# Gated-delta heads of a hybrid decoder step: the next head's convolutions, gates and norms are issued among the present head's work

## What is computed

```python
def causal_conv(u, buf, w):
    ...
    out = sum(xp[:, i:i + l] * w[i] for i in range(CONV_W))
...
    g = jnp.cumsum(log_a, axis=-1)
    diff = g[..., :, None] - g[..., None, :]
    decay_strict = jnp.exp(jnp.where(strict, diff, -jnp.inf))
    decay_causal = jnp.exp(jnp.where(causal, diff, -jnp.inf))
    kb = k * beta[..., None]
    lower = jnp.einsum('nbhik,nbhjk->nbhij', kb, k) * decay_strict
    a_mat = lower + jnp.eye(c, dtype=lower.dtype)
    ...
    sol = lax.linalg.triangular_solve(a_mat, rhs, left_side=True, lower=True)
    ...
    def step(s, xs):
        ...
        v_new = u_c - jnp.einsum('bhik,bhkv->bhiv', w_c, s)
        o = jnp.einsum('bhik,bhkv->bhiv', qd_c, s) + jnp.einsum('bhij,bhjv->bhiv', qk_c, v_new)
        s = s * gl_c[..., None, None] + jnp.einsum('bhjk,bhjv->bhkv', kd_c, v_new)
        return s, o
```

## Time and profile before

| | |
|---|---|
| median of 3 runs | 2871.9 us (2869.86 to 2873.43) |
| profiled execution | 2865.93 us, span 2864.2 us |
| PE busy | 2749.2 us, 96% of the span |
| DVE, POOL, ACT busy | 49%, 32%, 14% |
| chain of waits by engine | PE 85%, DVE 10%, ACT 2%, issue 2% |

### The profile page before, as it was taken

How to read it: one execution, slowest core, us unless ns; L and a number is a source line. 1 busy time by engine, 2 the same in 40 slices (tenths; PEclk the granted TensorE clock), 3 DMA queues, 4 the chain that set the end, 5 groups by cost and what they waited for, 6 DMA issues and landing times.

```text
span 2864.2 us, 42850 instructions
## 1 busy us (share of the span) xinstructions
PE 2749.2 (96%) x17350; PEld 2649.3 (92%) x17350; DVE 1411.2 (49%) x2523; ACT 406.7 (14%) x716; POOL 923.5 (32%) x1227
## 2 busy tenths in 40 slices
PE   8989889999999999999999999998999999999997
PEld 7877777898999999999999999997899999999997
DVE  5765756555576144261465335445575153261443
ACT  4333333222230000000001011112220000000001
POOL 3321221223234333333433323223233333343341
PEclk9999999999999999999999999999999999999999
DMA  3110110112311111111122122112311111111112
GB/s 125 52 53 16 53 53 16 60 53 69 107 38 45 47 50 45 45 52 45 45 65 91 51 67 77 54 52 76 106 35 47 45 48 49 45 45 52 45 45 74
DMA packets 46300, 160.22 MB, mean 56 GB/s; under 512 B 7198, under 2 KB 9118, under 8 KB 45102
## 3 DMA queue, kind: packets, MB, share of 16 engines
q1 hardware_dynamic: 30528, 111.20, 13.1%
q10 hardware_dynamic: 15598, 46.43, 4.5%
HBM read 138.97 MB, written 18.64 MB: 55 GB/s over the span
## 4 chain that ended last, share of the span: by engine, by line
PE 85%; DVE 10%; ACT 2%; issue 2%; DMA 1%; POOL 0%; DVEq 0%; ACTq 0%; POOLq 0%; SPq 0%
PE proj L376 71%; PE bank L453 10%; DVE s L899 2%; PE proj L431 1%; PE bank L450 1%; DVE s L797 1%; DVE x_lo L839 1%; DVE s L915 1%; PE bank L440 1%; DMA w_raw<-w_all 0%; PE bank L672 0%; DMA small<-rows_c 0%; DVE s L898 0%; DVE s L907 0%; DVE s L1016 0%
## 5 line engine op out<-in xcount | busy, mean ns | idle before, releaser
L376 PE MATMUL proj<-x_hi,w_hi 128*128 128x344 f32 x4716 | 1549.2, 328 | 54.2 <-DVE s L797 32.0
L376 PE MATMUL proj<-x_lo,w_hi 128*128 128x344 f32 x4716 | 1518.4, 322 | 0.0
L376 PE MATMUL proj<-x_hi,w_lo 128*128 128x344 f32 x4716 | 1517.8, 322 | 0.0
L376 PEld LDWEIGHTS proj<-x_hi,w_hi 128*128 128x128 f32 x4716 | 897.0, 190 | 79.2 <-issue 60.9
L376 PEld LDWEIGHTS proj<-x_lo,w_hi 128*128 128x128 f32 x4716 | 897.5, 190 | 1.6
L376 PEld LDWEIGHTS proj<-x_hi,w_lo 128*128 128x128 f32 x4716 | 896.8, 190 | 0.0
L311 POOL TENSOR_TENSOR w_lo<-w_raw,w_hi 128x256 fp32r<-128x256 f32 x808 | 665.2, 854 | 16.2
L307 POOL TENSOR_TENSOR pool_gate<-pool_gate 1x1 f32<-1x1 f32 x204 | 53.2, 261 | 1886.2 <-PE proj L376 1839.1
L1254 DVE TENSOR_TENSOR h<-h,proj 128x344 f32<-128x344 f32 x144 | 73.9, 513 | 453.1 <-PE proj L376 453.1
L1244 DVE TENSOR_TENSOR mlp_t<-proj,rbc 128x344 f32<-128x344 f32 x192 | 99.1, 516 | 269.6 <-PE proj L376 252.6
L308 POOL CAST w_hi<-w_raw 128x1024 fp32r<-128x1024 f32 x202 | 209.0, 1034 | 0.0
(11 more groups left out here) (270 smaller groups left out, 1900.6 us busy)
## 6 DMA issues: line engine op xcount, KB each, us to landing
w_raw<-w_all SPq DMA_DIRECT2D x204, 512.0 KB, 3.6
h<-x SPq DMA_DIRECT2D x8, 516.0 KB, 9.1
s<-rows_a ACTq DMA_DIRECT2D x8, 516.0 KB, 4.7
h<-x ACTq DMA_DIRECT2D x8, 516.0 KB, 6.9
h_spill<-h ACTq DMA_DIRECT2D x8, 516.0 KB, 2.6
h<-h_spill ACTq DMA_DIRECT2D x8, 516.0 KB, 6.6
y<-h ACTq DMA_DIRECT2D x8, 516.0 KB
sample_C<-state_c ACTq DMA_DIRECT2D x4, 1024.0 KB, 6.6
```

The costliest lines, as they stand in the source:

```text
L376: last = nc.tensor.matmul(PJ[:, tt, 0:TT], w[slot][:, k, :], x[:, k, tt * TT:(tt + 1) * TT], start=(at == 0 and j == 0), stop=(at == len(o ...
```

## The change

The delta heads become a pipeline of two. `mixer_ab` is split into `retention`, `delta_front` and `delta_main`. The front (26 steps: taps, silu, gate, norms) of head h+1 is issued among the places of the main part of head h, by a second table `DELTA_FRONT`; head 0's front is issued during a prologue of 12 places with 8 projection steps each. The projection stream is one generator over all delta tiles, two tiles further ahead than before: two tiles, then 96 steps in the prologue, 96 in each of heads 0 to 2, and 48 in the last head (`DELTA_LAST_FILL`), where before each of the four heads had 96 and four tiles stood ahead of them. The tiles of a head come in the order q, k, v, gate. Odd heads keep their convolved rows in other buffers (s[8] and two slices of the mixer output) than even heads.

Inside the head: the product of k and beta and the scaling of v by beta are gone; beta multiplies the triangular matrices (L1034 of the new program) and the new values of the scan (L1096) instead. The turned v is copied by ACT rather than by DVE. The causal mask is a constant of 0 and -200 that the exponents' instruction takes as a third operand (L1024), in the mLSTM heads too, where L1126 goes. The newest tap of q moves from DVE to ACT. The products of q with exp(g) move to level 2 of the inversion on DVE. The next head's decay row is loaded, and the sample states too, at level 2 on ACT; the beta rows are loaded once for the samples only. ACT loads function tables twice per head, before three times.

The core of the diff (lines that only rename are left out):

```diff
-DELTA_FILL = {"start": 7, "conv q": 14, "conv k": 10, "conv v": 8, "norm": 4, "operands": 12, "invert": 2,
-              "level 0": 0, "level 1": 0, "block": 0, "scan": 1, "state": 1, "residual": 1, "values": 1,
-              "sample": 2, "rows": 3, "output": 3, "outer": 0}
+DELTA_FILL = {"start": 8, "decay": 4, "invert": 6,
+              "block 1": 2, "block 2": 2, "block 3": 3, "block 4": 3, "block 5": 3, "block 6": 3,
+              **{f"state {c}": 4 for c in range(NC_)}, **{f"residual {c}": 1 for c in range(NC_)},
+              **{f"values {c}": 1 for c in range(NC_)}, "sample": 2, "rows": 3, "output": 6, "outer": 3}
+DELTA_FRONT = {"start": 1, "decay": 1, "block 3": 1, "block 4": 1, "block 5": 1, "block 6": 2,
+               "state 0": 1, "state 1": 1, "state 2": 2, "state 3": 2, "values 3": 2, "state 4": 1, "state 5": 1,
+               "state 6": 1, "residual 6": 1, "state 7": 1, "residual 7": 1,
+               "sample": 2, "rows": 1, "output": 1, "outer": 1}
+DELTA_LAST_FILL = {**DELTA_FILL, "start": 6, "decay": 4, "invert": 4,
+                   **{f"block {lv}": 2 for lv in range(1, LEVELS)}, **{f"state {c}": 2 for c in range(NC_)},
+                   **{f"residual {c}": 0 for c in range(NC_)}, **{f"values {c}": 0 for c in range(NC_)},
+                   "sample": 0, "rows": 0, "output": 4, "outer": 2}
+PROLOGUE = [f"prologue {i}" for i in range(12)]
+PROLOGUE_FILL = {place: 8 for place in PROLOGUE}
+PROLOGUE_FRONT = dict(zip(PROLOGUE, (2, 2, 2, 2, 2, 3, 2, 2, 2, 3, 2, 2)))
+FRONT_STEPS = 26
...
+            def delta_front(s, h):
...
+                for tmp in (tq, tk):
+                    pe.wait_ge(*n.awaited(front_to_pe))
+                    over_partitions(ones, tmp, "act")
...
+            def delta_main(s, h):
...
+                yield "start"
+                pe.wait_ge(*n.awaited(operands_in))
+                for half in range(2):
+                    per_chunk((4, 0)[half], "dve", half, lambda o, c: mm(o, chunk(k, c), chunk(k, c)))
+                for half in range(2):
+                    turned(1 + half, "act", v, half)
+                turned(3, "dve", k, 0)
+                per_chunk(2, "dve", 0, lambda o, c: mm(o, chunk(k, c), chunk(q, c)))
+                turned(1, "dve", k, 1)
+                yield "decay"
+                for half in range(2):
+                    pe.wait_ge(*n.awaited(to_pe))
+                    turned((4, 0)[half], "dve", LT, half)
+                yield "invert"
...
+            def along(main, stream, front, fill, steps):
+                for place in main:
+                    for _ in range(fill[place]):
+                        next(stream)
+                    for _ in range(steps.get(place, 0)):
+                        next(front)
...
+            stream = projections(T_AB, 4 * HEADS + 4, XA)
+            for _ in range(2 * NT * KC):
+                next(stream)
...
+            along(PROLOGUE, stream, delta_front(slots[0], 0), PROLOGUE_FILL, PROLOGUE_FRONT)
+            for h in range(HEADS - 1):
+                along(delta_main(slots[0], h), stream, delta_front(slots[0], h + 1), DELTA_FILL, DELTA_FRONT)
+            along(delta_main(slots[0], HEADS - 1), stream, None, DELTA_LAST_FILL, {})
...
+            def along(main, stream, front, fill, steps):
+                for place in main:
...
+                    issued[0] += fill[place]
+                    for _ in range(steps.get(place, 0)):
+                        next(front)
...
+                def tap(x, i):
+                    blk, sh = x * HEADS + h, 3 - i
...
+                    stt(dst[:, SEQ:TOK], hist, vcol(w + i), dst[:, SEQ:TOK], ALU.mult, ALU.add).then_inc(*n.stepped())
+                    step(stt(dst[:, sh:SEQ], src[:, 0:SEQ - sh], vcol(w + i), dst[:, sh:SEQ], ALU.mult, ALU.add))
...
+            def delta_main(s, h):
+                q, k, vv = conv_of(s, h)
...
+                yield "start"
+                v.wait_ge(g_in, n.awaited(g_in, 16)[1])
+                for c in range(NC_):
+                    last = stt(chunk(s[11], c), chunk(s[7], c), gcol[:, c, h:h + 1], causal, ALU.subtract, ALU.min)
+                last.then_inc(*n.made(to_act))
...
+                step(nc.vector.tensor_copy(cut(chunk(Dm, 0, NC_), NC_), rep(ident, NC_)))
+                yield "decay"
+                v.wait_ge(*n.awaited(to_dve))
+                for half in range(2):
+                    ps = take((4, 0)[half])
+                    for j in range(4):
+                        c = 4 * half + j
+                        last = stt(chunk(LT, c), chunk(ps, j), gcol[:, c, 32 + h:33 + h], chunk(s[11], c), ALU.mult, ALU.mult)
+                    last.then_inc(*done((4, 0)[half]))
+                    tell(to_pe)
...
+                    if lv == 2:
+                        v.wait_ge(*n.awaited(to_dve))
+                        tt_(s[10][:], q, s[7][:], ALU.mult)
+                        nc.vector.tensor_copy(glast[:, 0:NB], cut(s[7][:, 0:SEQ], NC_)[:, :, C - 1])
+                        step(nc.vector.tensor_copy(glast[:, NB:2 * NB], s[7][:, SEQ:TOK]))
                         tell(to_act)
...
+                    yield f"state {c}"
+                    ps = take(0)
+                    stt(resid[:], ps[:, 0:P], negeg[:, c, h:h + 1], chunk(s[17], c), ALU.mult, ALU.add).then_inc(*done(0))
+                    tell(to_pe)
+                    yield f"residual {c}"
+                    ps = take(1)
+                    ts_(vnew[:], ps[:, 0:P], gcol[:, c, 32 + h:33 + h], None, ALU.mult).then_inc(*done(1))
+                    tell(to_pe)
+                    yield f"values {c}"
...
+                    stt(chunk(s[11], c), chunk(grow, c), gcol[:, c, h:h + 1], causal, ALU.add, ALU.min)
...
-                step(tt_(cut(s[11][:, 0:SEQ], NC_), cut(s[11][:, 0:SEQ], NC_), rep(causal, NC_), ALU.mult))
...
+                    w = V_CONV + 4 * (x * HEADS + h) + 3
+                    act(conv[x], s[x][:], ACT.Copy, scale=vec[:, w:w + 1]).then_inc(*n.made(front_to_dve))
+
...
+                        a.wait_ge(*n.awaited(to_act))
+                        if h < HEADS - 1:
+                            row_to_all("rows_a", h + 1, s[7], g_in)
+                        if h:
+                            a.wait_ge(stored, n.awaited(stored, 32)[1])
+                        a.dma_start(s[9][:, 0:NB * P], io["state_a"][h]).then_inc(state_in, 16)
...
-    consts[:, K_CAUS:K_CAUS + P] = i[:, None] <= i[None, :]
+    consts[:, K_CAUS:K_CAUS + P] = np.where(i[:, None] <= i[None, :], 0, MASKED)
```

More of the change, by code:

```diff
@@ L556, in mixer_ab, with sample_tail @@
                     claim(3, "dve")
-                    publish(mm(MB[3][:, 0:P], chunk(Kd, c), vv), 3)
+                    publish(mm(MB[3][:, 0:P], chunk(Kd, c), vnew[:]), 3)
+                yield from sample_tail(s, small[:, NB:2 * NB])
+            def sample_tail(s, values):
                 yield "sample"
@@ L566, in mixer_ab @@
                 yield "rows"
-                sample_outer([small[:, NB:2 * NB] if delta else samp[:, 0:NB]])
+                sample_outer([values])
                 yield "output"
@@ L976, in mixer_ab @@
[L976 to L989 removed]
+                    v.wait_ge(*n.awaited(front_to_dve))
@@ new lines, in delta_main @@
+                    yield f"block {lv}"
+                    if lv == LEVELS - 1:
+                        v.wait_ge(*n.awaited(to_dve))
+                    for half in range(2):
+                        ps = take(half)
+                        if lv == LEVELS - 1:
+                            e = cut(chunk(E, 4 * half, 4), 4)[0:64, :, 64:128]
+                            tt_(e, e, cut(ps[0:64, 0:256], 4), ALU.subtract).then_inc(*done(half))
+                            continue
+                        d = every_other(chunk(Dm, 4 * half, 4), lv, 0)
+                        tt_(d, d, ps[:, 0:256].rearrange("p (n b) -> p n b", b=1 << lv), ALU.subtract).then_inc(*done(half))
+                        tell(to_pe)
+                        tell(to_act)
@@ L1065, in mixer_ab @@
[L1065 to L1073 removed]
+                yield from sample_attention(q, k)
@@ L1074, in mixer_ab @@
+                sample_rows()
+                step(nc.vector.tensor_copy(vv[:, SEQ:TOK], sm[7]))
                 tell(to_act)
@@ L1308, in _ @@
             v.wait_ge(proj_drained, NT)
-            first = projections(s, T_AB, 0, 4)
+            stream = (third_ for j in range(4 * HEADS + 4) for third_ in project_steps(T_AB + j, s[j % 4]))
             a = s[12][0:HEADS, :]
@@ L1312, in _ @@
             n.settle()
-            next(first)
+            next(stream)
             v.wait_ge(*n.awaited(to_dve))
@@ L1322, in _ @@
             tell(to_act)
-            for _ in first:
-                pass
+            for _ in range(2 * NT - 2):
+                next(stream)
             for half in range(2):
@@ new lines, in output_norm, with along, retention @@
+            def output_norm(s, OT):
+                n.settle()
+                a.wait_ge(*n.awaited(to_act))
```

(9 more changed lines are left out.)

744 lines of the change are left out of this document (408 added, 336 removed).

## The result

| | before | changed |
|---|---|---|
| median | 2870.9 us (4 runs, 2868.3 to 2873.4) | 2825.6 us (4 runs, 2823.4 to 2827.2) |
| profiled execution | 2865.93 us, span 2864.2 | 2827.23 us, span 2825.3 |
| end of the fourth delta head | 519.7 us | 476.1 us |

The ratio is 0.9849, 95% interval [0.9837, 0.9861]: 43 us faster by the ratio, 45.3 by the medians. The forecast was 2841 with a range of 2812 to 2864; the gain by the medians is half as large again as the 30.5 us forecast. The two profiled executions differ by 38.7 us only, because the one of before lies at the low end of its kernel's runs (2864.8 to 2876.4 over all calls); up to the end of the delta heads they differ by 43.6.

A forecast was written before the change was run, and what follows sets the result against it. PE bounds the kernel (96% busy), its reducible waits lying in the delta heads behind late drains. Work plus waits and clock put their end at 491.2, saving 28.5; mLSTM saves 2.0; 2871.9 - 30.5 = 2841 us, range 2812 to 2864.

The forecast's parts named there:

- Prologue: Before head 0: begins at 61.6 us, 49.0 of work and 1 of waits, ends at 111.6.
- Start, 4.0 us a head: Head's start: DVE's chain of 12.3 us to the matrices' first half outlasts PE's 10.4 of work; waits 4.0 a head.
- Levels and scan: PE's waits per delta head: 5.5 us in the inversion levels, 3.7 in the scan chunks.
- Last head: Fourth delta head: 48 steps and one sum, 58.5 us of work and 25.4 of waits, ending at 487.2.
- Clock, 4 us: Delta heads: about 12 us were lost to the lower clock before; with shorter waits 4 kept, giving 491.2.
- Rival B: Lower clock from a head's start to its levels' end: 92 us more, 2933 us; chance 0.08.
- The rule of the Trainium skill: PE's brief idling between matmul groups makes the clock swing; scan and levels at the lower level, 2933 instead of 2841.
- mLSTM heads, 2.0 us: mLSTM heads: the causal product goes, behind which PE waited twice, 2.2 us in all; saves 2.0.
- the signs that were named: Drain waits gone, PE 0.93 to 0.95 busy, heads about 98 us, largest waits behind L1034 and residual, clock 0.98 or more.
- Rival A: Front steps delay inversion and scan on DVE: 5 us more exposed in each of heads 0 to 2, 2856; chance 0.18.
- Rival C: Chains outside the levels covered: scan loses nothing, start 3 less a head, clock stays up; 2814 us; chance 0.14.
- Rival D: No overlap: PE's wait for the next head's norms replaces the drains' wait; time and chance counted in A's.

The follow-up runs named there:

- the run beside the matched steps: The changed kernel as it is, run again on the same chip as the matched steps: 2828.0 us, ratio to the kernel before 0.9847.
- the matched steps: Changed kernel with ACT's column copy ahead of level 2's DMA issues and projection steps moved to where PE waits: 2819.6 us, run again 2822.6 us.
- the first experiment: Changed kernel with the next head's front, but for its first step, at one place in the tail: 2893.5 us, 1.0089 of the kernel before.
- the mask's own run: Kernel before with only the causal mask as a constant in the exponents' instruction and both mask products gone: 2871.86 us against 2871.89, ratio 1.0005.
- the first two experiments: Changed kernel with the front at one place, 2893.5 us; then with the old arrangement of steps and front but the new arithmetic, 2886.4 us.
- the tiles shifted: Changed kernel with the projection stream 16 steps further ahead, so POOL's split falls on the exponents at a head's start: 2832.6 us, ratio to before 0.9871.

## Why the prediction was right, and where it was off

The direction, the mechanism and the range were right; the gain was put too low by a third. By the steps of the sum, up to the end of the fourth delta head (491.2 forecast, 476.1 measured):

- *Prologue.* Forecast to begin at 61.6 and last 50.0 us; it began at 59.5 and lasted 48.6: 3.5 us in all. Some 2 us at its beginning are luck. Between 30 and 40 us the profiled execution of before was granted 0.83 and that of the changed kernel 1.00; the second trace of the changed kernel (the run beside the matched steps) has 0.83 there too, and reaches the prologue's norm sums at 103.06 instead of 101.10. The 1 us of waits charged for the prologue did not come: PE is busy for 48.60 of its 48.60 us.
- *Start, 4.0 us a head: the step that failed.* The windows of heads 0 to 2 give 10.5 to 10.7 us of waits over 84.7 of work, against 13.2. At the start of each one wait of 0.3 us is left. In the last head, charged 6, the start took 2.2: 12.3 us of work in the 14.5 from 394.04 to the first product of the inversion at 408.52. So the four starts were charged 2, 4, 4 and 6 us and took about 3 together, and this term alone is 13 of the 15.1 us. The price of the exponents was taken from L915, whose eight instructions stood beside POOL's split; L1103's 2.13 us was likewise such a price, and its successor took 1.46 in head 1. The lower bound that the text named, 0.35 us for an instruction, was nearer: the eight of head 1 took 0.34 each and 2.18 together. The chain was 9.5 us long instead of 12.3, and PE's 10.4 covered it.
- *Levels and scan.* 5.5 and 3.7 a head were forecast; by the prices of the sum, head 1 lost about 5 in each, together about 10, 1 more than forecast. Four of the levels' gaps are in the rows above; with 3.70 us of work in a level of three steps, 0.45, 1.20 and 0.83 are left, and 1.39 ahead of level 3: right within some tenths, though for the taps' sake more than for the round trip's. The longest in the scan, 0.73 us, stood behind the third tap with its three copies, the first of which was held up (last section).
- *Last head.* 83.9 us forecast with no loss to the clock in it, 82.1 measured with one of about 4 (next point): so 19 to 20 us of waits over 58.5 of work, against 25.4. The start is most of the difference, the levels took 3.9 against 6.1, and the scan was right: a chunk of two steps takes 3.38 us, 2.06 of it work.
- *Clock, 4 us.* Heads 0 to 2 were granted 1.00 throughout, but the last head was not. Its scan and the stretch behind it (windows of the changed kernel):

```profile
434.50:461.50 27.00, 20.06 (x124) 16.81 (x122) 9.67 (x29) 2.22 (x8) 0.00 (x0) 1.00 0.02 7
461.50:471.80 10.30, 8.66 (x34) 8.25 (x35) 4.45 (x14) 1.06 (x1) 0.00 (x0) 0.50 0.01 2
```

  In this scan, with two steps a chunk, PE stands idle for 6.9 of 27 us in short waits, 16 of them (0.28 and 0.50 us) behind DVE; then 10.3 us were granted the lower level. Half of the 8.7 us that PE was busy there, about 4, is an estimate of the loss. That the 4 us came out is luck: the sum charged them for short waits in all heads, and they fell in one place that it did not name. In the second trace of the changed kernel the last head is granted 0.96. Rival B, and the price of 92 us that hung on it, did not come: the 18 waits of this kind in heads 0 to 2, 0.8 us or less each, left the clock at 1.00, and the waits of 7 to 11 us in the first experiment came with 0.92 and 0.89. For B the prediction names two stretches at 0.50; the earlier trace rows shows one. The rule of the Trainium skill, page "TensorE: Matmul & The Clock Gate", section "A second HAM failure mode: psum-queue depth-cycling", does not describe heads 0 to 2. The end of the last head may be a case of it; no run here tells.
- *mLSTM heads, 2.0 us.* Not confirmed. The wait behind L1127 has no counterpart after, but it was gone in the mask's own run too, which came out at 1.0005, and the profiled pair lost 5 us again behind the delta heads. Those stretches differ by as much from trace to trace: 2345 to 2351 us from the end of the fourth head to the end of the span, over all kernels here.

Of the signs that were named, the drain's waits went, PE is busy for 0.95 of heads 0 to 2 and a head takes 95 us. The largest wait left in them is not behind L1034 or the residual but behind ACT's copy at level 3, 1.39 us.

Rival A (DVE's order) did not come: the scan lost about 1 us a head more than it was charged, not 5. Rival C comes nearest: the start is covered and the clock stays up in three heads, and the scan is not covered. Rival D did not come either: no norm sum of the front is among PE's waits. That beta's place and the copies on ACT had a part in the gain was not tried; the first two experiments only show that all of the new arithmetic, with the front in one place or in blocks, ends slower than before.

## What to carry to other kernels

Where one engine's long block of row work delays the drains that another engine needs, cutting the block into single instructions and laying them into the waits of the neighbouring stage can gain what shortening it does not: here 43 us, where the same shorter arithmetic in one place or in blocks gained nothing. Steps of the stream belong to the places that get the row work: taken out of the levels, they cost 17 to 19 of these us. An arithmetic saving should be looked up in the timeline first: the mask's product had stood in a wait for ACT and was worth nothing. And a mean of a group is a price only for the same neighbours: look at the smallest, the median and the largest of one instruction before using it for another place.

## What was not expected of the hardware

The same small DVE instruction takes two to three times as long while POOL splits weights: eight exponents took 1.66 and 4.37 us in the kernel before, 2.18 and 5.05 in the changed kernel and with the tiles shifted, and each time the longer one lay under POOL's L311 or L340. The spread of the eight exponents of head 1 (the view of a single source line; shortest, median, longest in ns), in the changed kernel and with the tiles shifted, is

```profile
L1024 DVE SCALAR_TENSOR_TENSOR s<-s,gate_cols,consts x8: 339/340/347, 208.0 to 209.8; 128x128 f32<-128x128 f32 x8
L1024 DVE SCALAR_TENSOR_TENSOR s<-s,gate_cols,consts x8: 341/809/1251, 214.9 to 219.6; 128x128 f32<-128x128 f32 x8
```

In the timeline of DVE, two neighbours of the second group stand under the split:

```profile
217.15 0.81 DVE L1024 SCALAR_TENSOR_TENSOR s<-s,gate_cols,consts 128x128 f32<-128x128 f32 x1
217.88 0.81 DVE L1024 SCALAR_TENSOR_TENSOR s<-s,gate_cols,consts 128x128 f32<-128x128 f32 x1
```

They begin 0.73 us apart, and a piece of the split takes 0.73 (four in 2.93): each seems to wait for a piece. Three of the eight take 0.34, five 0.81 to 1.25. The Trainium skill, page "SBUF — State Buffer", section "Who interferes with whom", says that a DVE instruction with two inputs in SBUF contends with a GpSimd instruction that reads SBUF, because its second input comes through a read port that the two share. The same section calls this contention "an exclusive lock". The traces agree: an exponent alone takes 0.34 us, and 0.81 where one gets through for each piece.

A copy of 128x3 shows the same beside POOL's cast. In the scan of head 1 of the changed kernel it took 1.01 us, and 0.17 in an earlier chunk; it is the copy behind the third tap, ahead of PE's wait of 0.73 us (timelines of DVE and POOL):

```profile
275.31 1.01 DVE L968 COPY conv_out_rows<-s 128x3 f32<-128x3 f32 x1
275.27 1.03 POOL L337 CAST w_hi<-w_raw 128x1024 fp32r<-128x1024 f32 x1
```
